# Dot products first, gate products second: the order of a tick on VectorE

## The reference

```python
h = layer_norm(DN_ALPHA * x + mix, ln1_g, ln1_b)
h = layer_norm(DN_ALPHA * h + peer(h, peer_wq, peer_keys1, peer_keys2, peer_u, peer_v), ln2_g, ln2_b)
```

```python
ug = u[expert]
vg = v[expert]
act = jax.nn.gelu(jnp.einsum('td,thkd->thk', xb, ug).astype(jnp.float32), approximate=False)
return jnp.einsum('thk,thkd->td', (gate * act).astype(xb.dtype), vg)
```

## Time and profile before

| | us |
|---|---|
| median of 3 runs | 1748.22 |
| lowest, highest | 1747.89, 1752.08 |
| the profiled execution | 1746.99 |
| its span in the profile | 1745.2 |

### The profile page before, as it was taken

The page is one execution under the profiler, slowest core; times in us unless marked ns, Lnnn a source line. Parts: engine busy times, 40 slices in busy tenths (PEclk is TensorE's granted clock), DMA queues, the critical chain, the costliest instruction groups (busy, mean ns, idle before and its releaser), DMA issues.

```text
span 1745.2 us, 20306 instructions
## 1 busy us (share of the span) xinstructions
PE 1402.6 (80%) x7309; PEld 654.4 (37%) x7309; DVE 1039.9 (60%) x2599; ACT 496.5 (28%) x1239; POOL 795.7 (46%) x818
## 2 busy tenths in 40 slices
PE   8999998889899778879889989788788945566554
PEld 7644554347533323333357433234333311111110
DVE  3423364257686663843677792874925799854555
ACT  1031553012122344631222113454422222221111
POOL 0010073025331675643445323675734467777773
PEclk9999998999999888889999999789998986866887
DMA  8985475769999999999999999999999999999996
GB/s 290 365 269 171 157 229 170 263 241 409 409 409 409 404 409 409 378 378 383 398 409 408 409 409 385 367 409 389 384 378 392 330 378 410 409 410 409 409 409 277
DMA packets 202792, 625.20 MB, mean 358 GB/s; under 512 B 16632, under 2 KB 43960, under 8 KB 202508
## 3 DMA queue, kind: packets, MB, share of 16 engines
q0 software_dynamic: 112784, 410.17, 60.1%
q1 hardware_dynamic: 89908, 213.74, 33.4%
HBM read 611.62 MB, written 12.23 MB: 357 GB/s over the span
## 4 chain that ended last, share of the span: by engine, by line
PE 46%; DVE 18%; DMA 17%; POOL 9%; issue 5%; ACT 5%; SPq 0%; DVEq 0%; POOLq 0%; ACTq 0%
PE banks L705 18%; POOL BIG L609 9%; PE banks L678 9%; DVE BIG L1501 7%; DMA wbuf<-in_w_in_dram 6%; DMA BIG<-in_peer_v_dram,BIG 6%; DMA BIG<-in_peer_u_dram,BIG 5%; PE banks L646 5%; PE banks L771 4%; ACT BIG L1124 3%; PE banks L745 2%; PE banks L1018 1%; PE banks L975 1%; ACT L1124 1%; DVE BIG L1849 1%
## 5 line engine op out<-in xcount | busy, mean ns | idle before, releaser
L646 PE MATMUL banks<-BIG 64*64 64x512 f32 x3072 | 455.3, 709 | 214.0 <-DMA BIG<-in_peer_v_dram,BIG 118.2
L609 POOL DMA_INDIRECT BIG<-in_peer_v_dram,BIG x384 | 368.2, 959 | 437.8 <-PE banks L646 346.0
L1501 DVE CUSTOM_DVE_ANT_0 BIG<-BIG,banks 128x1024 f32<-128x1024 f32 x384 | 459.1, 1217 | 167.4 <-DMA BIG<-in_peer_u_dram,BIG 164.1
L609 POOL DMA_INDIRECT BIG<-in_peer_u_dram,BIG x384 | 367.1, 956 | 269.8 <-DVEq L1892 114.1
L705 PE MATMUL banks<-wbuf,BIG 128*128 128x512 f32 x832 | 385.8, 618 | 16.4 <-DMA wbuf<-in_w_in_dram 8.5
L646 PEld LDWEIGHTS banks<-BIG 64*64 64x64 f32 x3072 | 107.6, 147 | 515.0 <-issue 287.7
L1124 ACT ACTIVATE BIG<-banks 128x512 f32<-128x512 f32 (+5 forms) x255 | 131.4, 544 | 439.8 <-PE banks L678 133.1
L705 PEld LDWEIGHTS banks<-wbuf,BIG 128*128 128x128 f32 x832 | 159.4, 197 | 237.0 <-issue 204.7
L1124 ACT ACTIVATE BIG<-cst,small 128x64 f32<-128x64 f32 (+1 forms) x480 | 142.1, 349 | 347.1 <-DVE small L1490 345.0
L678 PE MATMUL banks<-wbuf,BIG 128*128 128x512 f32 x320 | 151.3, 629 | 2.5 <-ACT BIG L1124 2.5
L1124 ACT ACTIVATE small<-small 128x2 f32<-128x2 f32 (+1 forms) x204 | 41.3, 204 | 383.5 <-DVE small L1501 380.3
(11 more groups left out here) (169 smaller groups left out, 1004.7 us busy)
## 6 DMA issues: line engine op xcount, KB each, us to landing
wbuf<-in_w_in_dram SPq DMA_DIRECT2D x108, 1024.0 KB, 11.2
wbuf<-in_w_ssm_br_dram SPq DMA_DIRECT2D x24, 1024.0 KB, 5.9
wbuf<-in_peer_wq_dram SPq DMA_DIRECT2D x24, 1024.0 KB, 7.8
wbuf<-in_w_attn_br_dram SPq DMA_DIRECT2D x12, 1024.0 KB, 8.7
wbuf<-in_w_out_dram SPq DMA_DIRECT2D x12, 1024.0 KB, 7.3
out_s_ssm_dram<-BIG SPq DMA_DIRECT2D x16, 512.0 KB, 3.8
BIG<-in_peer_u_dram,BIG POOLq DMA_INDIRECT x384, 9.3
BIG<-in_peer_v_dram,BIG POOLq DMA_INDIRECT x384, 9.2
```

The source lines that it names most:

```text
L609: pool.indirect_dma_start(slot, None, table, bass.IndirectOffsetOnAxis(ap=eidx[:, col:col + 1], axis=0)).then_inc(done, 16)
L646: last = mm(acc[i][64 * half:64 * half + 64, :], dg[rows, :], vslot[k][rows, 512 * half:512 * half + 512], start=(b % BLOCKS == 0 and j == 0),
L1501: nc.vector.tensor_tensor_reduce(uslot[s], uslot[s], normed[:, :], 1.0, 0.0, ALU.mult, ALU.add, dots[k % 2][:, j:j + 1]).then_inc(dot_done, 1)
```

## The change

In VectorE's tick the lines that form w of block k-1 move from the front to behind the dots of block k. The copy of the normed vector at a tile's first block stays ahead of the dots.

```diff
--- before.py
+++ after.py
@@ -1484,10 +1484,6 @@
                 b = k - 2
                 if b and b % BLOCKS == 0:
                     add_experts(b // BLOCKS - 1)
-                if 1 <= k <= TOTAL:
-                    dve.wait_ge(gelu_done, k)
-                    at = (k - 1) * WB
-                    tt(w8[(k - 1) % 2], gl[(k - 1) % 2], gate[:, at:at + WB], ALU.mult).then_inc(w_ready, 1)
                 if k < TOTAL and k % BLOCKS == 0:
                     dve.wait_ge(h_ready, k // BLOCKS + 1)
                     if k:
@@ -1500,6 +1496,10 @@
                         dve.wait_ge(u_in[s], 16 * (k // RING + 1))
                         nc.vector.tensor_tensor_reduce(uslot[s], uslot[s], normed[:, :], 1.0, 0.0, ALU.mult,
                                                        ALU.add, dots[k % 2][:, j:j + 1]).then_inc(dot_done, 1)
+                if 1 <= k <= TOTAL:
+                    dve.wait_ge(gelu_done, k)
+                    at = (k - 1) * WB
+                    tt(w8[(k - 1) % 2], gl[(k - 1) % 2], gate[:, at:at + WB], ALU.mult).then_inc(w_ready, 1)
                 if k in LN2_AT:
                     last_norm(LN2_AT[k])
```

## The result

| | before | after |
|---|---|---|
| median, us | 1748.22 (1747.89 to 1752.08) | 1758.75 (1753.07 to 1761.60) |
| profiled execution, us | 1746.99 | 1757.47 |

The ratio is 1.0056, 95% interval 1.0035 to 1.0077: the changed kernel is slower by 0.0056 x 1748 = 9.8 us (the two medians lie 10.5 apart). The forecast was 1757.

What follows compares the result with a forecast made beforehand. DMA was taken as nearly always busy, except in two mixer stretches bound by engines waiting for each other. Terms 5.7 + 3.0 + 0.7 = 9.4 us on 1746.99 gave 1756.4, or 1757.6 from the median; stated 1757 us, range 1746 to 1769.

Steps and rivals of the forecast that it cites:

- What counts, and where: Mixers with experts: ScalarE leaves each tick later, costing time only where its very next work is waited for.
- The ten ticks named: Both passes with experts: four waited-for ticks each, 5.7 us together, and one scan-group tick with a table load, 3.0 together.
- the tick's exit: ScalarE's tick: it ends 0.71 us later where ScalarE had arrived early, as product and diagonals now precede gelu.
- the four places: Transposed mixture, first layer norm, group norm, exponentials ahead of state-space groups: 0.71 us each, in both passes, 5.7 us.
- The exposed table load: Scan group with one tick behind it: load no longer hidden under the dots, ramps 1.97 us later; 3.0 us over both passes.
- Half of it absorbed in pass 1: Scan group's table load in pass 1: DMA is full there, so only half counted, 1.0 us against 2.0 in pass 2.
- The end: Last block: its gelu stands behind the diagonals of the block ahead, with nothing left to absorb the delay; +0.7 us.
- What is gained: VectorE's saved waits between back-to-back ticks, in the last router: 4.8 us at most, counted as 0 because DMA is at its limit.
- No difference: Rival, whole kernel: DMA sets the time and absorbs all delays; 1747 to 1750 us, chance 0.26.
- Faster: Rival, last router's ticks and gathers: VectorE and u slots come free sooner; likeliest 1743 us, chance 0.10.
- Much slower: Rival, expert blocks: later diagonals hold TensorE, v slots and gathers, TensorE's wait well above 84.7 us; about 1771 us, chance 0.07.

Runs made afterwards that it cites:

- spots_only: Kernel before, with the dots first only in ten ticks, five in each pass with experts woven in; ratio to before 1.0037, 6.5 us slower.
- spots_back: Changed kernel (dots first), but with the product first as before in the same ten ticks of the two passes with experts; ratio to before 1.0012.
- norms_back: As spots_back, with the product first also in the two ticks ending in a second layer norm in the last router's pick; ratio to before 0.9999.
- gelu_first: Changed kernel, with ScalarE's gelu of block k put ahead of the diagonals of block k-1; ratio to before 1.0066.
- tail_only: Kernel before, with the dots first only behind the last mixer, from the last two parts of the last router's pick on; ratio to before 1.0024.
- early_before: Kernel before, with awaited ScalarE work (evictions, exponentials, ramps, group norm's root) put ahead of its tick in passes with experts; ratio 0.9957, 7.5 us faster.

## Why the prediction was right

- **What counts, and where.** Right. The ten ticks named bring 6.5 of the 9.8 us (spots_only), the two norms that were missed 0.0013 or 2.3 us (spots_back against norms_back, on two chips, with overlapping intervals), the rest about 1 us; the last two are below what these runs tell apart. What is shown is the ten places against all others; how the 6.5 us divide among the ten was not tried one by one.
- **The size of the tick's exit.** Too large: 0.71 forecast, 0.48 measured, so 3.8 us for the four places instead of 5.7. The step added up durations as if each instruction began where the one ahead ended; product and gelu start earlier.
- **The exposed table load.** 1.97 forecast, 1.90 measured. No drain shows: gelu starts 1.30 us after its load starts (736.72 to 738.02) and the root 1.30 after its own (1477.69 to 1478.99). The Trainium skill ("ScalarE: Activation LUTs", section "What ACT_TABLE_LOAD costs") gives 2.66 us for a load with its drain; this trace does not agree. What the step missed is that in pass 2 a second branch, TensorE's expert block at the lower clock, was as long (gelu_first). Half of it absorbed in pass 1 is not borne out at the place itself: in spots_only TensorE's matmul starts the full 1.90 us later there. Whether later gathers made up for part of it, no run shows.
- **The second layer norms.** Missed. The search went through the mixers, and these two ticks lie in the router's pick. It is the same mechanism with the load in the open at one of them: 1.91 + 0.49 = 2.4 us of waiting, which the time of the whole does not tell from none.
- **The end.** 0.7 forecast, nothing measured: from the read of the last dots to L1474 it is 5.03 us before (1728.55 to 1733.58) and 5.05 after (1738.99 to 1744.04). The last diagonals, at 1740.09, are hidden under TensorE's block ahead of them, at work since 1739.82. So the tick's exit was 1.9 us too large, this term 0.7, and the norms, 2.4 us, were missing: that the sum came out within half a microsecond is luck in part.
- **What is gained.** Right that it comes to nothing, and for the reason given, as far as one trace shows it (tail_only): saved waits for gelu in the router's pick became waits for u rows.
- **Rivals.** "No difference" holds, within 3 us, for the 180 ticks of norms_back, the tail among them, not for the places. "Faster" had the saving right and what follows it wrong. "Much slower" had the sign that it named, TensorE's wait far above 84.7 us, but that sign was no proof: the wait took the place of one for v rows, 203 us together before, 242 after, and GpSimd's wait behind it grew only from 346.0 to 379.5 us. Its mechanism is not nothing either: in one scan group it holds TensorE as long as the load does (gelu_first).

## What to carry to other kernels

When a piece of work moves behind another on one engine, follow not that engine but the next one: what it could do early and now does late stands between its last input and whatever others wait for. The price is paid at the few places where someone stands idle on that next work, and can be read there from one wait each; a wait that grows over the whole span may only have changed its releaser. The cure follows from the same reading: put the awaited work ahead of the step, as early_before did.

## What the runs showed of the hardware

A single profiled pair is worth little for sums over a span here. Before any expert block runs, where the change has no part, the changed kernel is 3.4 us ahead (367.37 against 370.74 at the same L678). Between 540 and 553 us it loses 5.0, from 1.8 ahead (539.22 against 540.99) to 3.2 behind (552.53 against 549.30), in a run of matmuls of the input projection in which TensorE waits for nothing. The second part of that run, before and after (table of stretches):

```profile
544.00:549.30 5.30, 5.30 (x14) 2.15 (x13) 5.05 (x19) 0.59 (x2) 0.00 (x0) 1.00 1.02 408
```

```profile
544.30:552.50 8.20, 8.20 (x13) 3.23 (x12) 2.00 (x8) 0.68 (x3) 0.00 (x0) 0.64 0.89 330
```

TensorE was granted 1.00 in the one and 0.64 in the other, so part of the latter at the lower of its two levels, 1.2 GHz, though it had been at work in both (after: 10.88 of the 13 us from 526 to 539, at clock 1.00).

A lower clock that comes back at the same place in every kernel with a long wait there is another matter. In the scan groups of pass 2, where VectorE runs the dots first in a tick, TensorE waits 3.3 us for diagonals. There are 17 such waits (3.32 to 3.35 us) in the seven traces that have them, and behind each the block takes 2.5 to 3.2 us, or two blocks 5.0 to 6.5. Where the product goes first, the wait there is 1.05 us or less and the block behind it takes 1.95. In pass 1, with waits of 2.6 us, some blocks are slow and some are not. So the later diagonals do cost TensorE time in these groups. How much of that reaches the time of the whole is not shown, but norms_back, with two of the 17, is no slower than the kernel before (0.9980 to 1.0018).

Only offsets from one event to the next inside a place came out alike in both passes and in every kernel that keeps the order of ScalarE's tick and places (2.16 or 2.17 with the product first there, 2.64 with the dots first; 3.19 and 5.09); totals needed the repeated runs.
